# Mixer projections moved into the steps of the latent attention, and the gated products of the expert loop taken one weight tile earlier

## The chip, the core and the metric

One core of one Trainium2 chip. Engines run their own instruction streams and meet through semaphores: TensorE (PE, its weight loads PEld), VectorE (DVE), ScalarE (ACT), GpSimd (POOL), and SyncE (SP), which issues most transfers. The metric is device time in microseconds of one launch, a median of runs.

## What is computed

Two models, one behind the other, on 512 tokens of width 1024. The first has two layers; the second has one, with 32 experts. Only what lies around the change is shown.

```python
def token_mixers(h, cos, sin, w_in, ...):
    proj = h @ w_in
    (sc_b, sc_c, sc_h, gq, gk, gv, gg, ga_f, ga_b, cq, ckv, kr, cfm_in) = jnp.split(proj, ...)
    y_a = sc_b * depthwise_conv(sc_c * sc_h, w_sc_conv)              # 3 taps
    ...  # gated linear attention over gq, gk, gv with decays from ga_f, ga_b -> o
    y_b = o * jax.nn.silu(gg)
    qm = (rms_norm(cq, g_mla_q) @ w_mla_uq)                          # 4 heads of 64 + 32
    kvm = (rms_norm(ckv, g_mla_kv) @ w_mla_ukv)                      # 4 heads of 64 + 64
    y_c = blocked_attention(q_c, k_c, v_c, ...)                      # 4 heads x 4 blocks of 128 queries
    a, gate = jnp.split(cfm_in, 2, axis=-1)
    u = depthwise_conv(a * jax.nn.sigmoid(gate), w_cfm_dw)           # 31 taps
    y_d = jax.nn.silu(layer_norm(u, ...))
    return concatenate(rms_norm of y_a, y_b, y_c, y_d) @ w_out

def run_block(args):                                                 # 128 slots of one expert
    hb = x_pad[toks] @ w1[e] + b1[e]
    g_part = jnp.minimum(hb[..., ::2], 7.0)
    u_part = jnp.clip(hb[..., 1::2], -7.0, 7.0)
    act = g_part * jax.nn.sigmoid(1.702 * g_part) * (u_part + 1)
    return act @ w2[e] + b2[e]
```

## The kernel before

All activations lie channel by channel: a tile is 128 channels by 512 tokens, and hT, the input of a layer, has eight of them. Weights come through one ring of eight tiles of 512 KB (RING, TILE); SP waits for a tile's slot (L393) and loads the next tile (L395). Each program of an engine is one stream in written order, so the order of the lines is the order of the work. Values are named in a table of marks: `when("probs", l, i)` is the count that the semaphore of an engine has reached when that value is there. TensorE's results go to eight banks that are handed out in turn (`bank`); a bank is taken again when the engine that read its last holder has said `free`.

A mixer layer (DEPTH is 2) is ordered like this before the change:

- TensorE (from L627 to L730): the projections of PROJ in the order a0, a1, gate0, gate1, misc (with a second use of its tile, kswap), ckv, cq0, cq1, q, k, then the four banks of gv (two tiles), then b0, b1, c0, c1, h0, h1, gg0, gg1. `project` is eight products of a weight tile with hT. Then the sums of squares of ckv and cq (`norm`), one modulation tile for the second model (`modulation(("kv", l))`, 16 matmuls of two columns), the keys and values of the latent attention (knope, mv), the queries (qh, qswap) and the decays' inputs (la).
- The attention has 16 steps, i = head * 4 + block. In step i TensorE issues the scores of step i + 1, waits for the probabilities of step i and transposes them; after every fourth step it waits for the copied transposes and multiplies them with the values (yc). ScalarE keeps the scores (L1216), takes the exponential (L1220) and copies the transposes of step i - 1 (L1201). VectorE takes the row maximum (L1775), the reciprocal of the row sum (L1778) and scales (L1781).
- VectorE runs the 31 taps of the wide convolution (L1659, two channel tiles, so 62 operations) and the 3 taps of the short one under the projections.
- ScalarE copies each projection out of its bank (`keep`, L1157).
- Behind the attention, TensorE has ten modulation tiles (`modulation(("gla", l, 0))`), while VectorE and ScalarE make the decays and their products for the gated linear attention (from L1785, L1229); TensorE then waits for the first of them (kdec, L1833).

The expert loop has 32 laps, one block of 128 slots each, 24 weight tiles a lap (MOE_TILES). A weight is used as two parts: ScalarE rounds the tile (`round_tile`, L1530) into w_hi, VectorE subtracts that from the tile (`rest_of_tile`, L2311) into w_lo. There are six pairs of them (SPLITS); tile t is rounded when product t - 6 has been made (s_freed). SP may load tile t + 8 when VectorE has done with tile t (s_lo). Products 0 to 7 of a lap fill one pair of banks, 8 to 15 the next; each of them goes through `sigmoid` (L1552) and `swiglu` (L2333 to L2342), is turned by TensorE (act_turned, L1057) in the middle of the eight products that follow, and is split (`round_act`, `rest_of_act`, L2348). Products 16 to 23 use the result. The middle of a lap stands on ScalarE and VectorE like this:

```python
                for t in range(SPLITS, KD + SPLITS):      # 6 to 13
                    rest_of_tile(i, t)
                swiglu(0)                                 # waits for product 7
                for t in range(KD + SPLITS, KD + SPLITS + 2):
                    rest_of_tile(i, t)
                rest_of_act(0)
```

Of the kernel before, what the change touches and what calls it, by code (L numbers as in the profile page):

```python
# [104 lines left out]
SLOT = {n: i for i, n in enumerate(PROJ)}  # L105

# [25 lines left out]
def build(nc, io, marks, found):  # L132
    with ExitStack() as ctx:
# [107 lines left out]
        z_la, cneg, e_la, dtmp = spare("c0"), spare("h0"), spare("cq0"), spare("gate0")  # L241
# [311 lines left out]
        def _(pe):  # L553
# [51 lines left out]
            def used(n=1):  # L605
                state["pending"] += n
# [27 lines left out]
            def project(name, ready=None):  # L634
                w = tile().rearrange("p (k m) -> p k m", m=P)
                chunks(name, lambda k: w[:, k, :], lambda k: hT[:, k, :], KD, ready=ready)
                used()

# [3 lines left out]
            for l in range(DEPTH):  # L642
                project(("proj", l, PROJ[0]), ready=("norm_out", ("in",) if l == 0 else ("ln2", l - 1)))
                for name in PROJ[1:4]:
                    project(("proj", l, name))
                w = tile().rearrange("p (k m) -> p k m", m=P)
                chunks(("proj", l, "misc"), lambda k: w[:, k, :], lambda k: hT[:, k, :], KD)
                chunks(("kswap", l), lambda k: w[:, k, 32:128], lambda k: hT[:, k, :], KD, 96)
                used()
                for name in PROJ[5:10]:  # L650
                    project(("proj", l, name))

                w0 = tile().rearrange("p (k m) -> p k m", m=MIX)
                w1 = tile().rearrange("p (k m) -> p k m", m=MIX)
                for b in range(TB):
                    out = bank("gv", l, b)
                    for k in range(KD):
                        mm(out[:, 0:MIX], hT[:, k, b * P:(b + 1) * P], (w0 if k < 4 else w1)[:, k % 4, :],
                           k == 0, k == KD - 1, *(("gv", l, b) if k == KD - 1 else ()))
                used(2)  # L660
                for name in PROJ[10:]:
                    project(("proj", l, name))
# [36 lines left out]

                pe.wait_ge(dve_done, when("keys", l))  # L700
# [410 lines left out]
        def _(act):  # L1111
# [41 lines left out]
            for l in range(DEPTH):  # L1153
# [6 lines left out]
                keep("a0"), keep("a1"), keep("gate0", ACT.Sigmoid), keep("gate1", ACT.Sigmoid)  # L1160
                keep("misc")
                for i, name in enumerate(("ckv", "cq0", "cq1")):
# [6 lines left out]
                act.wait_ge(pe_done, when("full", "proj", l, "q"))  # L1169
                act.wait_ge(act_done, did.n)  # L1170
                nc.scalar.activation(proj[:, SLOT["q"], :], bank_of("proj", l, "q")[:], ACT.Copy,
                    scale=DK ** -0.5).then_inc(act_done, did.up(("free", "proj", l, "q"), ("proj", l, "q")))
                keep("k")
                for b in range(TB):
                    act.wait_ge(pe_done, when("full", "gv", l, b))
                    act.wait_ge(act_done, did.n)
                    nc.scalar.activation(vtok[:, b, :], bank_of("gv", l, b)[:, 0:MIX], ACT.Copy).then_inc(act_done,
                        did.up(("free", "gv", l, b), ("gv_kept", l, b)))
                for name in PROJ[10:16]:
                    keep(name)  # L1180
# [1381 lines left out]
```

## Time and profile before

| | |
|---|---|
| median of three runs | 3957.78 us (3948.6 to 3963.21) |
| profiled execution | 3951.65 us, span 3949.9 us |
| PE busy | 3554.2 us (90%) |
| PEld busy | 2481.5 us (63%) |
| DVE busy | 2409.6 us (61%) |
| ACT busy | 1733.2 us (44%) |
| POOL busy | 509.8 us (13%) |
| HBM read, written | 588.45 MB, 29.36 MB |

Layer 0 of the first model runs from about 39 to 928 us, layer 1 to about 1818, the second model's mixer to about 2640, and the expert loop from there to the end. Busy time is that of the records; matmuls overlap, so their busy time isn't their pace. A granted clock of 1.00 is 2.4 GHz, 0.50 is 1.2 GHz. The DMA share is the mean over 16 engines. "Idle before" names the time that an engine waited ahead of an instruction, and what ended the wait.

### The profile page before, as it was taken

What the parts mean: (1) busy time and instruction counts of PE and PEld (TensorE: products, weight loads), DVE (VectorE), ACT (ScalarE), POOL (GpSimd) and SP (SyncE); (2) the same over time, 40 slices, a digit from 0 to 9 for tenths busy, and PEclk for the clock granted to TensorE, in tenths of its full rate; (3) what the DMA queues carried; (4) which work ended last, traced back from release to release, by engine and by line L of the source; (5) the groups of instructions that cost most, each with busy time, mean ns of one, the idle gap of its engine ahead of it and who ended that gap; (6) DMA issues with size and microseconds to landing.
All of it is one profiled execution on the core that took longest, in us unless ns stands there. A gap on an engine that the chain in (4) does not pass through costs nothing.

```text
span 3949.9 us, 43762 instructions
## 1 busy us (share of the span) xinstructions
PE 3554.2 (90%) x13692; PEld 2481.5 (63%) x13692; DVE 2409.6 (61%) x2911; ACT 1733.2 (44%) x2333; POOL 509.8 (13%) x625
## 2 busy tenths in 40 slices
PE   7978799999978799997888899959999999999996
PEld 3437468874437468875554554457777777777774
DVE  5334355654334355653335774168888898988885
ACT  2134132332144142333221113047787877777874
POOL 0000000000000000000000000023434343434340
PEclk9975799999975899997999999979999999999998
DMA  4202123322202122322111002259999999999994
GB/s 172 74 16 80 53 75 96 96 91 69 75 16 80 55 76 94 96 91 75 38 42 48 22 1 91 75 192 339 345 336 346 336 362 332 353 332 349 335 354 161
DMA packets 167840, 619.37 MB, mean 157 GB/s; under 512 B 18512, under 2 KB 18640, under 8 KB 167024
## 3 DMA queue, kind: packets, MB, share of 16 engines
q1 hardware_dynamic: 156768, 573.84, 40.8%
q0 software_dynamic: 10960, 44.04, 4.0%
q8 instruction: 70, 1.15, 0.1%
q14 instruction: 42, 0.34, 0.0%
HBM read 588.45 MB, written 29.36 MB: 156 GB/s over the span
## 4 chain that ended last, share of the span: by engine, by line
PE 61%; DVE 15%; DMA 9%; ACT 7%; issue 7%; POOL 0%; DVEq 0%; ACTq 0%; SPq 0%; POOLq 0%
PE bank L569 51%; DMA sb_ring<-in_w 8%; PE bank L1049 7%; DVE w_part L2311 3%; ACT w_part L1530 2%; DVE sb_rstd L1624 2%; DVE sb_work L2338 1%; DVE sb_work L2342 1%; DVE sb_work L2333 1%; PE bank L1057 1%; DVE sb_work L2335 1%; PE bank L1018 1%; ACT sb_work L1220 0%; DVE sb_work L2110 0%; DVE sb_turn_tables L2106 0%
## 5 line engine op out<-in xcount | busy, mean ns | idle before, releaser
L2311 DVE TENSOR_TENSOR w_part<-sb_ring,w_part 128x1024 fp32r<-128x1024 f32 x762 | 894.7, 1223 | 128.2 <-ACT w_part L1530 127.8
L1530 ACT ACTIVATE w_part<-sb_ring 128x1024 fp32r<-128x1024 f32 x762 | 772.5, 1053 | 145.5 <-PE bank L1049 86.3
L1049 PE MATMUL bank<-w_part,xg_hi 128*128 128x512 f32 x2048 | 570.1, 400 | 0.0
L569 PE MATMUL bank<-h_hi,split_part 128*128 128x512 f32 x1408 | 443.5, 400 | 8.3 <-ACT h_hi L1319 8.3
L1049 PEld LDWEIGHTS bank<-w_part,xg_hi 128*128 128x128 f32 x2048 | 387.1, 190 | 90.7
L569 PE MATMUL bank<-sb_work,sb_ring 128*128 128x512 f32 (+4 forms) x864 | 330.3, 538 | 16.5 <-DVE sb_modv L1614 10.5
L1049 PE MATMUL bank<-w_part,xg_lo 128*128 128x512 f32 x1024 | 323.6, 397 | 0.0
L569 PEld LDWEIGHTS bank<-h_hi,split_part 128*128 128x128 f32 x1408 | 267.4, 190 | 74.8 <-issue 8.4
L569 PE MATMUL bank<-sb_work 128*128 128x64 f32 (+6 forms) x992 | 253.2, 461 | 42.1 <-DVE sb_work L1833 22.8
L1049 PE MATMUL bank<-w_part,act_hi 128*128 128x512 f32 x1024 | 284.7, 400 | 0.1
L569 PEld LDWEIGHTS bank<-sb_work,sb_ring 128*128 128x128 f32 (+3 forms) x864 | 163.1, 190 | 179.8 <-issue 159.1
L569 PE MATMUL bank<-sb_hT,sb_ring 128*128 128x512 f32 (+1 forms) x608 | 265.4, 599 | 11.4 <-ACT sb_hT L1140 11.4
L569 PE MATMUL bank<-h_lo,split_part 128*128 128x512 f32 x704 | 272.4, 394 | 0.0
L569 PE MATMUL bank<-act_hi_ff,split_part 128*128 128x512 f32 x704 | 229.0, 407 | 5.7 <-DVE act_lo_ff L1940 5.7
L442 POOL DMA_DIRECT2D sb_work<-in_ctx x1 | 0.6, 592 | 1798.2 <-PE bank L569 1798.2
L569 PEld LDWEIGHTS bank<-sb_work 128*128 128x128 f32 (+3 forms) x992 | 159.1, 248 | 105.9 <-issue 46.0
L1049 PEld LDWEIGHTS bank<-w_part,xg_lo 128*128 128x128 f32 x1024 | 194.6, 190 | 47.1
L1312 ACT ACTIVATE split_part<-sb_ring 128x1024 fp32r<-128x1024 f32 x136 | 142.7, 1052 | 176.7 <-PE bank L569 176.7
L569 PEld LDWEIGHTS bank<-sb_hT,sb_ring 128*128 128x128 f32 (+1 forms) x608 | 115.9, 191 | 158.9 <-issue 156.5
L1049 PEld LDWEIGHTS bank<-w_part,act_hi 128*128 128x128 f32 x1024 | 187.5, 188 | 40.0 <-issue 0.5
L490 POOL TENSOR_TENSOR sb_work<-sb_work 128x1 f32<-128x1 f32 x126 | 97.3, 773 | 666.8 <-ACT sb_work L1588 394.0
L1348 ACT ACTIVATE sb_work<-bank 128x512 f32<-128x512 f32 x88 | 52.8, 600 | 294.8 <-PE bank L569 294.8
(331 smaller groups left out, 5055.9 us busy)
## 6 DMA issues: line engine op xcount, KB each, us to landing
sb_ring<-in_w SPq DMA_DIRECT2D x768, 512.0 KB, 7.1
sb_ring<-in_wstream SPq DMA_DIRECT2D x304, 512.0 KB, 3.5
y_rows<-sb_padc POOLq DMA_DIRECT2D x1, 4096.0 KB, 27.6
sb_xT<-in_x SPq DMA_DIRECT2D x1, 2048.0 KB, 11.5
x_rows<-sb_padc SPq DMA_DIRECT2D x1, 2048.0 KB, 22.6
residual<-sb_hT POOLq DMA_DIRECT2D x1, 2048.0 KB, 7.7
sb_hT<-residual POOLq DMA_DIRECT2D x1, 2048.0 KB, 8.0
x_rows<-sb_work SPq DMA_DIRECT2D x1, 2048.0 KB, 12.6
```

The lines of the kernel that those rows point to most:

```text
L490: nc.gpsimd.tensor_tensor(passed[:, n:n + 1], slot_row[:, 0:1], slot_row[:, 0:1], ALU.add).then_inc(moe_pool_done, turn_did.up())
L569: ins = nc.tensor.matmul(out, l, r, start=start, stop=stop)
L1018: ins = nc.tensor.transpose(out[:, k * P:(k + 1) * P], block_rows[:, (half * 4 + k) * P:(half * 4 + k + 1) * P], ident)
L1049: ins = nc.tensor.matmul(out[n][:], l[:, k, :], r[:, n * 512:(n + 1) * 512], start=False, stop=(k, p) == (KD - 1, 2))
L1057: ins = nc.tensor.transpose(banks[6 + half][:, k * P:(k + 1) * P], u_part[:, half, k * P:(k + 1) * P], ident)
L1312: nc.scalar.activation(split_hi[t % NSPLIT], ring[:, n % RING, :], ACT.Copy).then_inc(act_done, did.up(("w_hi", l, t)))
L1348: nc.scalar.activation(ubuf[:, i % 4, 1:T + 1], bank_of("up", l, c, v)[:], ACT.Copy).then_inc(act_done, did.up(("free", "up", l, c, v), (" ...
L1530: nc.scalar.activation(w_hi[t % SPLITS], ring[:, t % RING, :], ACT.Copy).then_inc(s_hi, 1)
L1624: nc.vector.reciprocal(out, out).then_inc(dve_done, did.up())
L2311: nc.vector.tensor_tensor(w_lo[t % SPLITS], ring[:, t % RING, :], w_hi[t % SPLITS].bitcast(F32), ALU.subtract).then_inc(s_lo, 1)
L2333: nc.vector.tensor_scalar(g_part, pairs[:, :, 0], SWIGLU_LIMIT, None, ALU.min).then_inc(moe_dve_done, turn_did.up(("g_part", half)))
L2335: nc.vector.tensor_scalar(u, pairs[:, :, 1], SWIGLU_LIMIT, -SWIGLU_LIMIT, ALU.min, ALU.max).then_inc(moe_dve_done, turn_did.up())
```

## The change

In the mixers, `project` now takes its weight tile by name, so that tiles can be used out of order. Ahead of the attention stand only ckv, cq0, cq1, misc, a0, the two norms' sums, then a1, gate0, gate1. The projection q goes right ahead of step 0, and the other ten stand in steps 0 to 8, 14 and 15 (BESIDE_AT), between the scores of step i + 1 and the wait for the probabilities of step i; gv takes two steps with two banks each. ScalarE keeps them one step later, ahead of copying the transposes (`keep_beside`); gg0 and gg1 it keeps behind the last step. The modulation tile goes into step 10. VectorE's 31 wide taps go into the steps, two taps (four operations) each, behind the scaling; the products of c and h and the short taps go into steps 11 to 14, and the product with b behind step 15. The buffer z_la moves from c0's place to the last two tiles of sq.

In the expert loop, `sigmoid` and `swiglu` of either half go ahead of one more weight tile: ahead of tile 13 and tile 21, which stood before them until now.

```diff
+GV_TILE = 10
+BESIDE_AT = {0: "k", 1: "gv0", 2: "gv2", 3: "c0", 4: "h0", 5: "c1", 6: "h1", 7: "b0", 8: "b1", 14: "gg0", 15: "gg1"}
+MOD_STEP = 10
...
-        z_la, cneg, e_la, dtmp = spare("c0"), spare("h0"), spare("cq0"), spare("gate0")
+        z_la, cneg, e_la, dtmp = sq[:, 6:8, :], spare("h0"), spare("cq0"), spare("gate0")
...
+            def project(l, name, ready=None):
+                i = SLOT[name]
+                w = loaded(in_layer + i + (2 if i >= GV_TILE else 0)).rearrange("p (k m) -> p k m", m=P)
+                chunks(("proj", l, name), lambda k: w[:, k, :], lambda k: hT[:, k, :], KD, ready=ready)
+                if name == "misc":
+                    chunks(("kswap", l), lambda k: w[:, k, 32:128], lambda k: hT[:, k, :], KD, 96)
                 used()
...
+                in_layer = state["stream"]
+                project(l, "ckv", ready=("norm_out", ("in",) if l == 0 else ("ln2", l - 1)))
+                for name in ("cq0", "cq1", "misc", "a0"):
+                    project(l, name)
                 norm(("kv", l), sq, 0, 1, ones, center=False)
                 norm(("q", l), sq, 1, 2, ones_mix, center=False)
+                for name in ("a1", "gate0", "gate1"):
+                    project(l, name)
+                state["stream"] = in_layer + len(PROJ) + 2
-                modulation(("kv", l))
...
+                project(l, "q")
                 pe.wait_ge(dve_done, when("keys", l))
...
                     if i + 1 < HEADS * TB:
                         scores(i + 1)
+                    if i in BESIDE_AT:
+                        if BESIDE_AT[i][:2] == "gv":
+                            token_values(l, int(BESIDE_AT[i][2]))
+                        else:
+                            project(l, BESIDE_AT[i])
+                    if i == MOD_STEP:
+                        modulation(("kv", l))
                     pe.wait_ge(dve_done, when("probs", l, i))
...
                     if i >= 1:
+                        if i - 1 in BESIDE_AT and BESIDE_AT[i - 1][:2] != "gg":
+                            keep_beside(i - 1)
                         turned_out(i - 1)
                 turned_out(HEADS * TB - 1)
+                keep("gg0", ACT.Silu), keep("gg1", ACT.Silu)
...
                         ALU.mult).then_inc(dve_done, did.up(("probs", l, i)))
+                    dve.wait_ge(dve_done, did.n)
+                    wide_taps(2 * i, min(2 * i + 2, CFM_TAPS))
+                    if i == HEADS * TB - 1:
+                        did.note("norm_in", ("cfm", l))
+                    if i == MOD_STEP + 1:
+                        modulated(("kv", l))
...
+                    if MOD_STEP + 1 < i < MOD_STEP + 5:
+                        dve.wait_ge(dve_done, did.n)
+                        short_taps(i - MOD_STEP - 2)
...
-                for t in range(SPLITS, KD + SPLITS):
+                for t in range(SPLITS, KD + SPLITS - 1):
                     rest_of_tile(i, t)
                 swiglu(0)
-                for t in range(KD + SPLITS, KD + SPLITS + 2):
+                for t in range(KD + SPLITS - 1, KD + SPLITS + 2):
                     rest_of_tile(i, t)
                 rest_of_act(0)
-                for t in range(KD + SPLITS + 2, 2 * KD + SPLITS):
+                for t in range(KD + SPLITS + 2, 2 * KD + SPLITS - 1):
                     rest_of_tile(i, t)
                 swiglu(1)
-                rest_of_tile(i, 2 * KD + SPLITS)
+                for t in range(2 * KD + SPLITS - 1, 2 * KD + SPLITS + 1):
+                    rest_of_tile(i, t)
                 rest_of_act(1)
```

ScalarE's loop changes in the same way, with round_tile and sigmoid.

## Rows read from the trace of the kernel before

**Rows 1.** The page, part 4: the chain that ended last, shares of the span

```profile
PE 61%; DVE 15%; DMA 9%; ACT 7%; issue 7%; POOL 0%; DVEq 0%; ACTq 0%; SPq 0%; POOLq 0%
```

**Rows 2.** Windows: stretch, length, busy of PE, PEld, DVE, ACT, POOL, clock, DMA, GB/s

```profile
39.00:186.00 147.00, 146.65 (x369) 70.50 (x370) 65.89 (x105) 23.38 (x37) 0.00 (x0) 0.98 0.20 68
...
217.15:294.30 77.15, 53.54 (x126) 20.48 (x124) 21.52 (x49) 35.20 (x68) 0.00 (x0) 0.71 0.04 14
1108.90:1183.00 74.10, 54.31 (x132) 21.40 (x130) 21.50 (x49) 35.69 (x69) 0.00 (x0) 0.70 0.04 15
```

**Rows 3.** Groups by form, 100 to 170 us: busy us, mean ns of one

```profile
L569 PE MATMUL bank<-sb_hT,sb_ring 128*128 128x512 f32 x132 | 57.0, 592 | 0.0
```

**Rows 4.** Timeline, 184 to 222 us: start, us, then the idle time before

```profile
186.76 1.28 ACT L1124 ACT_TABLE_LOAD   x1
...
188.06 1.49 ACT L1124 ACTIVATE sb_rstd<-bank,sb_consts 128x512 f32<-128x512 f32 x2
...
188.78 3.35 DVE L1624 RECIPROCAL sb_rstd<-sb_rstd 128x512 f32<-128x512 f32 x1 [9.81 <-ACT sb_rstd L1124]
...
193.18 5.32 PE L569 MATMUL bank<-sb_work,sb_ring 128*64 128x512 f32 x8 [2.87 <-DVE sb_work L1642]
```

**Rows 5.** Timeline, one attention step of layer 0

```profile
280.81 0.60 ACT L1216 ACTIVATE sb_work<-bank 128x512 f32<-128x512 f32 x1
280.86 0.66 PE L710 MATMUL bank<-sb_consts,sb_work 128*128 128x128 f32 x4 [1.80 <-DVE sb_work L1781]
...
281.44 0.69 DVE L1775 TENSOR_REDUCE sb_work<-sb_work 128x1 f32<-128x512 f32 x1 [0.64 <-ACT sb_work L1216]
282.17 0.72 ACT L1220 ACTIVATE sb_work<-sb_work 128x512 f32<-128x512 f32 x1 [0.75 <-DVE sb_work L1775]
...
283.28 0.49 DVE L1781 TENSOR_SCALAR sb_work<-sb_work 128x512 f32<-128x512 f32 x1
```

**Rows 6.** Timeline, VectorE: the wide convolution's taps behind the first

```profile
71.63 39.84 DVE L1659 SCALAR_TENSOR_TENSOR sb_work<-sb_padc,sb_cols,sb_work 128x512 f32<-128x512 f32 x60
```

**Rows 7.** Timeline behind the attention: modulation tiles, and the decay chain's ends

```profile
294.30 29.37 PE L569 MATMUL bank<-sb_csil,sb_ring 128*128 128x2 f32 x160
...
302.37 1.36 ACT L1229 ACTIVATE sb_work<-sb_work 128x512 f32<-128x512 f32 x2 [7.37 <-DVE sb_work L1790]
...
319.75 2.56 DVE L1833 SCALAR_TENSOR_TENSOR sb_work<-sb_work 128x1024 f32<-128x1024 f32 x2
```

**Rows 8.** Windows of the expert loop, columns as in rows 2

```profile
3000.77:3040.73 39.96, 37.70 (x173) 30.23 (x172) 35.58 (x37) 31.21 (x36) 16.64 (x20) 1.00 0.95 342
3022.00:3030.00 8.00, 8.00 (x37) 6.44 (x36) 7.78 (x8) 7.76 (x10) 0.34 (x1) 1.00 0.67 203
3000.00:3022.00 22.00, 19.75 (x93) 15.64 (x92) 20.52 (x23) 15.85 (x20) 14.23 (x17) 1.00 1.02 396
2640.00:3877.00 1237.00, 1173.25 (x5292) 940.78 (x5291) 1102.70 (x1120) 968.27 (x1086) 493.69 (x589) 0.99 0.95 342
```

**Rows 9.** Timeline of one lap: VectorE's idle moments and one gated product

```profile
3001.97 1.23 DVE L2311 TENSOR_TENSOR w_part<-sb_ring,w_part 128x1024 fp32r<-128x1024 f32 x1 [0.34 <-ACT w_part L1530]
...
3003.11 0.68 DVE L2333 TENSOR_SCALAR sb_work<-bank 128x512 f32<-128x512 f32 x1
...
3005.25 0.69 DVE L2342 TENSOR_TENSOR sb_work<-sb_work 128x512 f32<-128x512 f32 x1
...
3014.78 1.23 DVE L2311 TENSOR_TENSOR w_part<-sb_ring,w_part 128x1024 fp32r<-128x1024 f32 x1 [0.17 <-ACT w_part L1530]
...
3020.14 0.69 DVE L2348 TENSOR_TENSOR act_lo<-bank,act_hi 128x512 fp32r<-128x512 f32 x1 [0.24 <-ACT act_hi L1558]
...
3023.38 6.90 DVE L2311 TENSOR_TENSOR w_part<-sb_ring,w_part 128x1024 fp32r<-128x1024 f32 x6 [0.22 <-ACT w_part L1530]
```

**Rows 10.** Waits in the expert loop, 2640 to 3895 us: total, times, longest

```profile
PE bank L1057 <- DVE sb_work L2342: 66.6, 63, 2.3
...
DVE w_part L2311 <- ACT w_part L1530: 117.9, 161, 2.1
```

More of the change, by code:

```diff
@@ L632, in running, with token_values @@
                 mm(state[kind][:], ones_d, src[:, k, :], k == 0, k == KD - 1, *((kind, tag) if k == KD - 1 else ()))
-            def project(name, ready=None):
-                w = tile().rearrange("p (k m) -> p k m", m=P)
-                chunks(name, lambda k: w[:, k, :], lambda k: hT[:, k, :], KD, ready=ready)
-                used()
+            def project(l, name, ready=None):
[4 more added lines that the diff above has]
+                    chunks(("kswap", l), lambda k: w[:, k, 32:128], lambda k: hT[:, k, :], KD, 96)
+                used()
+            def token_values(l, first):
+                if first == 0:
+                    state["gv"] = [loaded(in_layer + GV_TILE + i).rearrange("p (k m) -> p k m", m=MIX) for i in range(2)]
+                w0, w1 = state["gv"]
+                for b in range(first, first + 2):
+                    out = bank("gv", l, b)
+                    for k in range(KD):
+                        mm(out[:, 0:MIX], hT[:, k, b * P:(b + 1) * P], (w0 if k < 4 else w1)[:, k % 4, :],
+                           k == 0, k == KD - 1, *(("gv", l, b) if k == KD - 1 else ()))
+                if first > 0:
+                    used(2)
             pe.wait_ge(s_in, 16 * 5)
@@ L1158, in keep @@
                         **kw).then_inc(act_done, did.up(("free", "proj", l, name), ("proj", l, name)))
-                keep("a0"), keep("a1"), keep("gate0", ACT.Sigmoid), keep("gate1", ACT.Sigmoid)
-                keep("misc")
                 for i, name in enumerate(("ckv", "cq0", "cq1")):
@@ L1168, in _ @@
                     keep(name)
[L1169 to L1180, printed above, removed]
-                keep("gg0", ACT.Silu), keep("gg1", ACT.Silu)
+                keep("misc")
+                keep("a0")
                 deviation(("kv", l), scale=1.0 / P)
                 deviation(("q", l))
+                keep("a1"), keep("gate0", ACT.Sigmoid), keep("gate1", ACT.Sigmoid)
                 for h in range(HEADS):
@@ L1209, in turned_out, with keep_beside @@
                             ACT.Copy).then_inc(act_done, did.up(("free", "yc", l, h), ("yc", l, h)))
+                def keep_beside(i):
+                    name = BESIDE_AT[i]
+                    if name[:2] == "gv":
+                        for b in range(int(name[2]), int(name[2]) + 2):
+                            act.wait_ge(pe_done, when("full", "gv", l, b))
+                            act.wait_ge(act_done, did.n)
+                            nc.scalar.activation(vtok[:, b, :], bank_of("gv", l, b)[:, 0:MIX],
+                                ACT.Copy).then_inc(act_done, did.up(("free", "gv", l, b), ("gv_kept", l, b)))
+                    else:
+                        keep(name)
+                keep("q", scale=DK ** -0.5)
                 for i in range(HEADS * TB):
@@ L1650, in conv @@
                 n = len(dst)
-                for j in range(taps):
+                for j in taps:
                     for c in range(n):
@@ L1772, in _, with wide_taps, short_taps @@
                         ALU.add).then_inc(dve_done, did.up(("free", "la", l, d)))
+                for c in range(2):
+                    dve.wait_ge(act_done, when("proj", l, f"gate{c}"))
+                    dve.wait_ge(dve_done, did.n)
+                    nc.vector.tensor_tensor(padc[:, c, 15:T + 15], proj[:, SLOT["a0"] + c, :], proj[:,
+                        SLOT["gate0"] + c, :], ALU.mult).then_inc(dve_done, did.up())
+                def wide_taps(j0, j1):
+                    conv([proj[:, SLOT["a0"] + c, :] for c in range(2)], lambda c: padc[:, c], range(j0, j1),
+                         lambda c, j: col(l, "cfm_w", c * CFM_TAPS + j))
+                def short_taps(j):
+                    conv([y[:, c, :] for c in range(2)], lambda c: pads[:, c], (j,),
+                         lambda c, j: col(l, "sc_w", c * 3 + j))
                 for i in range(HEADS * TB):
```

61 lines of the change are left out of this document (16 added, 45 removed).

## The prediction

> **What bounds the kernel now.** I read the chain that ended last first [rows 1]: TensorE holds 61% of it, VectorE 15%, and 9% is weight loads of the expert loop. So two places are worth a look: where TensorE's line is broken in the mixers, and where the loop waits.
>
> Mixers: the table by stretches of layer 0 [rows 2] shows projections with TensorE busy all of 147 us at a granted clock of 0.98, and then attention, 77.15 us in layer 0 and 74.10 in layer 1, with 53.5 busy at a clock of 0.71. The reader is to see both losses: 24 us idle, and much of the busy time at the lower of the two levels. The steps themselves are a chain [rows 5]: keep the scores (0.60), row maximum (0.69), exponential (0.72 and its read-out), scaling (0.49), transposes (0.66), then the next.
>
> Loop: 1237 us hold 31 laps of 39.9 us, with a DMA share of 0.95, TensorE busy 1173.25 us (94.8%) and VectorE 1102.70 (89.1%) [rows 8]. The waits [rows 10] name all that TensorE waited for there: 66.6 us for the gated product (L2342), 2.15 us a lap. VectorE waited 117.9 us (3.8 a lap) for rounded tiles. Three resources stand close together, so removing TensorE's wait need not be worth 2.15.
>
> **The change part by part, mixers.** I count one layer from 39.0 us to the start of the ten modulation tiles, 294.3 us: 255.3 us.
>
> One projection is 16 matmuls; 132 of them took 57.0 us [rows 3], so 6.9 us each. Before, 21 such units (two of them the value tiles, and one the second use of misc) give 144.9 of the 146.65 us [rows 2], with 1.8 for the cold start. After, nine stand ahead (ckv, cq0, cq1, misc twice, a0, a1, gate0, gate1): 62.1 + 1.8, and six matmuls of the two norms by the same row, 2.6: 66.5 us.
>
> The norms' square root, reciprocal (3.35 each) and scaling (0.7 each) left a hole [rows 4]: TensorE idles 2.87 before L569 at 193.18 and then runs eight matmuls in 5.32 us that take 3.4 at the full clock. After, a1, gate0 and gate1 (20.7 us) cover table load, root, two reciprocals and three scalings (1.3 + 1.4 + 6.7 + 2.2 = 11.6), so I cost them at nothing; without cover they would be 7 us. From 193.18 to the first kept score, 217.15, were 24.0 us; less 1.9 of cold clock 22.1. Then comes q, 6.9. So far 95.5 us.
>
> The steps: scores 0.86 (two matmuls), a projection 6.9, transposes about 0.5 apart, since they pipeline. That is 8.3 us on TensorE. Beside it VectorE has four taps at 0.66 (39.84 over 60) [rows 6], the maximum, a short reciprocal and the scaling, 4.0 us, and ScalarE some 2.7 (four operations of the kinds in [rows 5]). Both fit, so steps 0 to 8 take nine times 8.3, 74.3 us. Steps 3 and 7 add the head's values, 3.4 at full clock, and about 1.0 of waiting for the copied transposes, which stand behind a kept projection on ScalarE: 8.8.
>
> Steps 9 to 13 have no projection. Here the added taps do cost: VectorE must finish 2.7 us of them before the next maximum. Its loop is 2.7 + 0.7 + 0.8 + 0.9 = 5.2, where a step before took about 4.5. Steps 9 and 10 together 4.6 (the first is ready, and the modulation tile, 2.9 by the ten tiles' row [rows 7], runs beside). Step 11 takes 5.5 to its transposes; its values and step 12, behind the two products of pads (1.4), about 10; step 13 3.5. That makes 23.5, and 28 if the clock falls as it does in the steps now. I take 26. Steps 14 and 15: 8.3 + 7.4 + 1.0 + 3.4, and 2.5 for a cold first projection: 22.6. Steps together 131.7.
>
> New layer 95.5 + 131.7 = 227.2 against 255.3: 28.1 saved; layer 1, whose attention was 3.05 shorter, 25.0. Both 53.
>
> What is late next: after the steps the ten modulation tiles take 29.4 us, and the decay chain ends at 319.75 + 2.56 = 322.3, before the tiles' end at 323.7 [rows 7]. The chain starts from the last head's copy on ScalarE, as before; y's two products and the last taps run on VectorE under the values. But gg0 and gg1 with Silu now stand on ScalarE ahead of the decay's exponential: load 1.28, two copies 1.2, load 1.28, 3.8 us, inside the 7.37 us that ScalarE idled there. Nothing, then, with 1.4 us of slack behind it. The Trainium skill (ScalarE: Activation LUTs, What ACT_TABLE_LOAD costs) adds a drain of 1.38 us to every load of 1.28, which would speak against the extra switch. In this trace the root starts 0.02 us after its load ended (188.06 against 186.76 + 1.28) [rows 4], so the row decides; by the page 6.5 us would stand there, still inside.
>
> Of weight loads, the change moves order alone: the same tiles are asked of SP's queue, and in the steps, where the DMA share is now 0.04 [rows 2]. No cost.
>
> **The loop.** Product 7 frees both the slot that tile 13 is rounded into and the banks that the gated product reads. Before, rounding (1.06) and the rest on VectorE (1.23) of tile 13, and of tile 21, came first; now the product does, 2.85 us from the first minimum to the last multiplication (3003.11 to 3005.94) [rows 9]. If TensorE alone decided, its 2.15 us a lap [rows 10] would go. But VectorE does the same work: between its tile 12 and tile 24 it is full but for idle moments of 0.34, 0.17, 0.24 and 0.22 [rows 9], which the order closes, since each was a wait for ScalarE, and the gated product now fills it. That is 0.97 a lap. What starts a lap is tile 12 landing, and its load is issued when VectorE ends tile 4 of that lap, so VectorE's 0.97 is carried on through the ring. The other bound is TensorE's 2.15. The low bound is a loss, below. I take 1.0, nearest to VectorE's rows, because VectorE issues what DMA waits for: 31 laps, 31 us.
>
> Also late in this order: tile 13 and 21 are finished 2 to 2.7 us later, and the loads into their slots with them. Behind the waiting multiplication on VectorE are tiles 13 to 15; TensorE wants tile 13 three products later, and they are 1.4 us each.
>
> **Sum.** 53 + 31 = 84 us from the profiled 3951.65 (span 3949.9): 3868. The median of the runs shown is 6.1 higher, 3957.78, so I predict 3874.
>
> **Rivals.**
> - The loop doesn't move. For it: DMA is 1.02 in the full stretch (396 GB/s) and 0.95 over all [rows 8], so at most 2.7 us a lap is slack, and none if its low stretch is latency that comes back. Against: in that low stretch (0.67, 203 GB/s, 8 us) loads wait for VectorE. Time 3957.8 - 53 = 3905.
> - The loop gains all of TensorE's wait, 66.6. For: TensorE's own work is 37.7 in the lap from 3000.77 [rows 8] and it has no other wait. Against: of VectorE's 3.8 us of idle time a lap, 1.7 would then be all that is left beside its work of 35.6 to 36, and only 0.97 of it has a cause that goes away. 3957.8 - 53 - 67 = 3838. The Trainium skill (DMA: Bandwidth & Descriptors, Anatomy of one DMA) gives bytes over 436 GB/s for data movement; 342 GB/s over 39.9 us would then need 31 us and leave TensorE the bound, which is this rival. The full stretches here show 396, so the page's rate isn't reached, and the trace speaks half for it.
> - The steps don't hold their projections at full clock, or transposes and copies wait in the other engines' new order: a third of the mixer's gain, 18, with the loop's 31: 3909.
> - Slower: the ring starves. The ring has eight tiles; the loads behind tiles 13 and 21 go out 2.85 us later, right ahead of the stretch where DMA is already at 0.67. If the queue runs dry for it, each lap pays 2.85 and not 0: 88 us against 53, 3957.8 + 35 = 3993. It decides from the point where the load behind tile 21, then issued at about 3018.9, comes after the full stretch has ended; that stretch reaches to 3022 [rows 8], which leaves 3 us, some two tiles of 1.3 us at 396 GB/s.
> - The change doesn't do what it says: TensorE runs in order, and a projection put between scores and transposes only lengthens a step by its 6.9 if the chain of the next step can't run under it. Then all is moved, nothing hidden, and the taps come on top: 3950. Against: scores of step i+1 are issued ahead of the projection, and everything they need is two steps old.
>
> **How the numbers follow.** Forecast 0.42 (its own range 3850 to 3895); loop unmoved 0.22; full loop 0.14; steps a third 0.10; starved ring 0.06; nothing hidden 0.06. The range takes in the loop unmoved and the steps' third, with the mixer's bounds of 35 to 60 us (all cold in steps 9 to 13 on the one side, values unwaited on the other), and half of the full loop: 3843 to 3915. 0.5% is about what a measurement of this kernel can tell, some 20 us: faster 0.88, same 0.06, slower 0.06.
>
> **What would show it.** Right: the distance from the layer's first projection to the modulation tiles near 227 us, granted clock near 1 over steps 0 to 8 and falling in 9 to 13, steps at 8.3 us; no hole before L569's first keys; the wait for the last decay product unchanged. In the loop: TensorE's wait for the gated product under 1 us a lap, a lap of 38.9, VectorE's small idle moments gone, DMA share 0.97 or more. Wrong: VectorE's taps ahead of a maximum with TensorE idle in steps 0 to 8; the modulation tiles followed by a wait; laps of 39.9 with ScalarE waiting longer for tiles (DMA), or above 40 with the low DMA stretch longer (starved).

## The result and the profile after

The changed kernel takes 3822.1 us, median of 4 runs (3815.6 to 3830.2), against 3956.9 for the kernel before (4 runs, 3948.6 to 3963.2): a ratio of 0.967, with an interval of 0.9644 to 0.9697. The forecast was 3874 with a range of 3843 to 3915. So the direction was right and the size was not: the time lies 52 us below the forecast and 21 below the range.

The profiled execution took 3815.60 us (span 3813.8), 136.1 less than the profiled 3951.65 of before. Two stamps of the expert loop divide this sum. The first is the first gated product, the second the last one of a first half. The rows are the answer for that line in the kernel before and then after: operation and count, shortest/median/longest in ns, first and last start. The last start is that of a second half; the last first half starts at 3877.0 before and at 3743.1 after.

```profile
L2333 DVE TENSOR_SCALAR sb_work<-bank x64: 678/684/686, 2642.8 to 3891.3; 128x512 f32<-128x512 f32 x64
```

```profile
L2361 DVE TENSOR_SCALAR sb_work<-bank x64: 676/682/687, 2589.5 to 3755.7; 128x512 f32<-128x512 f32 x64
```

The loop begins 53.3 us earlier, which is the mixers' part (forecast 53). From there the first halves' products of the 32 turns are 1234.1 us apart before and 1153.6 after: 39.81 us a lap against 37.21, 2.60 less, 80.6 over 31 laps (forecast 31). The last 2.2 lie behind them. The error is in the loop.

**Mixers.** Windows of the changed kernel, columns as in [rows 2]. In order: the projections ahead of the attention; the norms' stretch with a1, gate0 and gate1 in it; steps 0 to 8; steps 9 to 12; the last steps.

```profile
39.00:106.00 67.00, 66.97 (x151) 28.96 (x152) 25.83 (x35) 17.20 (x25) 0.00 (x0) 0.97 0.17 55
106.00:142.46 36.46, 36.46 (x90) 15.19 (x89) 18.25 (x29) 8.90 (x17) 0.00 (x0) 1.00 0.18 58
142.46:218.00 75.54, 73.67 (x229) 39.07 (x228) 35.75 (x61) 22.89 (x45) 0.00 (x0) 1.00 0.18 56
218.00:244.00 26.00, 15.04 (x55) 7.32 (x54) 16.47 (x30) 9.89 (x20) 0.00 (x0) 0.74 0.12 41
244.00:265.45 21.45, 20.76 (x52) 8.63 (x50) 12.94 (x22) 4.02 (x8) 0.00 (x0) 0.92 0.14 43
```

Against the attention of [rows 2], where TensorE was busy 53.54 of 77.15 us at a granted clock of 0.71, the reader sees nine steps in which it is busy 73.67 of 75.54 us at 1.00. The hole of [rows 4] is gone (36.46 of 36.46). The loss sits where the steps have no projection: 11 us idle, clock 0.74.

**Behind the attention.** Timeline rows that answer to [rows 7]: start, length, then the idle time before.

```profile
265.45 31.65 PE L572 MATMUL bank<-sb_csil,sb_ring 128*128 128x2 f32 x160
266.22 1.28 ACT L1169 ACT_TABLE_LOAD   x1
267.51 1.28 ACT L1169 ACTIVATE sb_work<-bank 128x512 f32<-128x512 f32 x2
268.88 1.28 ACT L1245 ACT_TABLE_LOAD   x1
...
273.51 1.35 ACT L1245 ACTIVATE sb_work<-sb_work 128x512 f32<-128x512 f32 x2 [3.35 <-DVE sb_work L1818]
...
290.88 2.56 DVE L1861 SCALAR_TENSOR_TENSOR sb_work<-sb_work 128x1024 f32<-128x1024 f32 x2
...
296.95 8.66 PE L572 MATMUL bank<-sb_work 128*128 128x64 f32 x40
```

The two gate copies and two table loads stand in ScalarE's idle time, of which 3.35 us remain of 7.37. The decay chain ends at 293.4, the modulation tiles at 297.1: TensorE goes on without a wait. But the tiles themselves last 31.65 us, where they lasted 29.37.

**Loop.** Windows, columns as in [rows 2]: the whole loop, and one lap, to be read against the last and the first row of [rows 8].

```profile
2588.00:3743.00 1155.00, 1153.42 (x5278) 938.41 (x5277) 1096.26 (x1118) 961.26 (x1085) 448.83 (x586) 1.00 1.00 365
2963.00:3000.07 37.07, 37.07 (x171) 30.24 (x170) 35.28 (x37) 30.92 (x36) 14.26 (x19) 1.00 1.00 368
```

TensorE is busy 99.9% of the time, DMA has a share of 1.00 (0.95 before), VectorE 94.9% (89.1%). The waits of the loop, in total us, times, longest, answer to [rows 10]:

```profile
PE bank L1069 <- DVE sb_work L2370: 1.2, 3, 0.6
```

66.6 us have become 1.2. The timeline of one lap, beside [rows 9], shows the product ahead of a tile (2963.05 to 2965.88), and the transposes of the activation coming when its result is there, with no idle time before them:

```profile
2963.05 0.68 DVE L2361 TENSOR_SCALAR sb_work<-bank 128x512 f32<-128x512 f32 x1
...
2965.19 0.69 DVE L2370 TENSOR_TENSOR sb_work<-sb_work 128x512 f32<-128x512 f32 x1
2965.80 3.49 DVE L2339 TENSOR_TENSOR w_part<-sb_ring,w_part 128x1024 fp32r<-128x1024 f32 x3
...
2967.01 0.60 PE L1069 MATMUL bank<-sb_consts,sb_work 128*128 128x128 f32 x4
```

### The profile page after: what moved, and what is told of

It is laid out like the page before. It is cut to its first block, busy times and chain, and to the rows that moved or that the text cites. A ratio compares the mean times of both kernels' runs of the same rounds, so it can differ in the third digit from the quotient of the medians.

```text
span 3813.8 us, 43797 instructions
## 1 busy us (share of the span) xinstructions
PE 3506.0 (92%) x13692; PEld 2476.4 (65%) x13692; DVE 2405.6 (63%) x2911; ACT 1727.9 (45%) x2334; POOL 465.9 (12%) x625
## 4 chain that ended last, share of the span: by engine, by line
PE 54%; issue 20%; POOL 10%; DVE 8%; ACT 4%; POOLq 2%; DMA 1%; SPq 0%; DVEq 0%; ACTq 0%
PE bank L572 53%; POOL pick L538 2%; DVE sb_rstd L1640 2%; POOL sb_work L493 2%; POOL y_rows L544 1%; POOL sb_work L499 1%; POOL picks_e L500 1%; POOL sb_work L530 1%; POOLq L506 1%; POOL sb_work L532 1%; POOLq L505 1%; DVE sb_work L2138 0%; DVE sb_turn_tables L2134 0%; POOL sb_work L527 0%; DVE sb_work L2162 0%
## 5 line engine op out<-in xcount | busy, mean ns | idle before, releaser
L572 PE MATMUL bank<-sb_work 128*128 128x64 f32 (+6 forms) x992 | 231.6, 438 | 45.8 <-DVE sb_work L1861 22.8
L1926 DVE TENSOR_TENSOR split_part<-sb_ring,split_part 128x1024 fp32r<-128x1024 f32 x136 | 165.8, 1220 | 19.9 <-ACT split_part L1328 19.8
```

The lines of the kernel that those rows point to most:

```text
L572: ins = nc.tensor.matmul(out, l, r, start=start, stop=stop)
L1926: nc.vector.tensor_tensor(split_lo[t % NSPLIT], ring[:, n % RING, :], split_hi[t % NSPLIT].bitcast(F32), ALU.subtract).then_inc(dve_done, ...
```

## The experiments

Two theories stand against each other in the expectations. **T**: TensorE sets the lap, and the lap lost exactly the time for which TensorE had stood before the activation's transposes. **V**: VectorE's order sets it, by way of the ring: a tile landing at the start of a lap, its load issued when VectorE frees the slot. A lap below is the mean distance of first halves' products over 31 laps of one profiled execution. Four kernels with the new loop order (after, its repetition, e2 and e5) have means of 37.21, 37.32, 37.23 and 37.41 and the same median, 37.08, so 0.2 in a mean says little and the median is given where it matters. A gap is the distance from the start of the last matmul ahead of the transposes to the first of them, less the 0.23 us at which matmuls follow each other.

**The two parts alone.** The loop's edits undone in the changed kernel, and the loop's edits alone in the kernel before.

```diff
 e1: the changed kernel with the loops of ScalarE and VectorE as before (the edits below, backwards)
 e2: the kernel before, with these edits
-                for t in range(SPLITS, KD + SPLITS):
+                for t in range(SPLITS, KD + SPLITS - 1):
 (and the other three ranges of the change, on both engines)
```

> The changed kernel with the expert loop's order as it was; the mixers' part stays. The question is how the 136 us that the profiled executions differ by (3951.65 to 3815.60) divide. The first gated product of the loop starts 53.3 us earlier in the changed kernel (2642.84 against 2589.52), so both theories expect 53 us less than the kernel before, a ratio of 0.9865, laps of 39.8 us again and a DMA share of 0.95 in the loop. If the ratio is under 0.98, some of what I put down to the loop belongs to the mixers.

> The kernel before with the loop's new order alone. Theory T (TensorE is the clock of a lap: its products, 37.1 us, plus the gaps between starts ahead of its transposes, 1.87 and 0.71 us beyond the usual 0.23) expects laps of 37.1 to 37.2 and 80 us less, a ratio of 0.980. Theory V (the prediction's: VectorE's idle moments of 0.97 a lap, passed on through the ring) expects laps of 38.9 and 31 us less, 0.992; under it the missing 50 us would have to come from the mixers' part.

Before was 3945.2 (7 runs) here. Mixers alone: 3896.9, ratio 0.9876 (0.9860 to 0.9893), 48 us less; its lap is 39.70. Loop alone: 3874.1, ratio 0.9824 (0.9808 to 0.9841), 71 us less, and a lap of 37.23 against 39.81. The two gains, 119 us, are less than the 135 of both together above (130 when the changed kernel was run again, below), and each interval reaches some 7 us to either side; the profiled executions give 45 for the start of the loop in e1 (2598.1) and 80 for the laps in e2. The mixers' forecast of 53 is met within these bounds, on their low side. The loop's part is less than T's time by about 10 us and far more than V's 31: V as the prediction had it has fallen.

**The halves of the loop.** The product of the first half moved alone (e3), and of the second alone (e4).

```diff
 e3
-                for t in range(SPLITS, KD + SPLITS):
+                for t in range(SPLITS, KD + SPLITS - 1):
                     rest_of_tile(i, t)
                 swiglu(0)
-                for t in range(KD + SPLITS, KD + SPLITS + 2):
+                for t in range(KD + SPLITS - 1, KD + SPLITS + 2):
 e4
-                for t in range(KD + SPLITS + 2, 2 * KD + SPLITS):
+                for t in range(KD + SPLITS + 2, 2 * KD + SPLITS - 1):
                     rest_of_tile(i, t)
                 swiglu(1)
-                rest_of_tile(i, 2 * KD + SPLITS)
+                for t in range(2 * KD + SPLITS - 1, 2 * KD + SPLITS + 1):
+                    rest_of_tile(i, t)
```

> The kernel before with only the first half's gated product (and its sigmoid) one weight tile earlier. Theory T: the gap of 1.87 us ahead of the first half's transposes goes and the 0.71 of the second stays: laps of 37.9, 58 us less, ratio 0.985. Theory R (the ring: the gain is only there when both halves fill the stretch in which the DMA engines are at 0.67, since loads wait for VectorE there): less than the half's own gap, laps near 39, 25 us less, 0.994.

> The kernel before with only the second half's gated product one weight tile earlier. Theory T: the 0.71 us gap goes: laps of 39.1, 22 us less, ratio 0.9944. Theory R: the second half stands right ahead of the stretch where DMA is at 0.67 (3022 to 3030 in the lap shown), so this half gives the larger part: laps of 38.5 or less, 40 us or more, under 0.990.

e3: ratio 0.9872 (0.9854 to 0.9891), lap 38.03. e4: 0.9934 (0.9917 to 0.9951), lap 38.91. The waits of the loop, first of e3, then of e4:

```profile
PE bank L1057 <- DVE sb_work L2342: 23.1, 32, 1.4
```

```profile
PE bank L1057 <- DVE sb_work L2342: 44.8, 30, 2.1
```

| kernel | lap, us | gap, first half | gap, second half |
|---|---|---|---|
| before | 39.81 | 1.69 | 0.70 |
| e3, first half moved | 38.03 | 0.02 | 0.88 |
| e4, second half moved | 38.91 | 1.56 | 0.00 |
| after | 37.21 | 0.03 | 0.03 |

Each half takes its own gap away and the lap follows: -1.78 and -0.90, together -2.68 against -2.60 for both. The parts add up. The gaps together fall by 1.49 in e3 (where the second half's grows by 0.18), by 0.83 in e4 and by 2.33 in the changed kernel. Most of what e3 and the changed kernel gain beyond that is the clock. In the 31 laps of the kernel before, TensorE's granted clock is at the lower level, 0.50, in four short stretches, 13.7 us in all; one of them:

```profile
2966.00:2969.00 3.00, 3.00 (x8) 2.32 (x8) 2.88 (x4) 1.99 (x2) 2.85 (x5) 0.50 1.07 407
```

At half speed 13.7 us cost 6.9 us, 0.22 a lap. e4 has four such stretches too, e3 and the changed kernel have none in these laps. With 0.22 added where they went, the sums are 1.71, 0.83 and 2.55 against laps shorter by 1.78, 0.90 and 2.60. That speaks for T.

**Less to load, in both kernels.** Every fourth tile of the expert loop is loaded by half (512 of 1024 columns), so an eighth of the weights is not read, and the output is not the reference's. If the lap waits for data, it shortens.

```diff
+                n = TILE // 2 if t % 4 == 0 and signal is s_lo else TILE
-                sp.dma_start(ring[:, t % RING, :], src).then_inc(s_tile[t % RING], 16)
+                sp.dma_start(ring[:, t % RING, 0:n], src[:, 0:n]).then_inc(s_tile[t % RING], 16)
```

> The kernel before with only half of every fourth weight tile loaded in the expert loop (the output is then not the reference's): 6 half tiles a lap, 1.57 of some 13.6 MB, 12% of a lap's traffic. The step of the prediction that is on trial said that a lap starts when its tile 12 lands. If it does, the lap of 39.8 us shortens by at least half of the 4 us of traffic, to 38 or less. Theory T (TensorE's work and its two gaps make the lap; the DMA stretch at 0.67 is only what they leave over): laps stay at 39.7 to 39.8, and the DMA share falls to 0.84.

> The same cut of traffic in the changed kernel, where the DMA share stands at 1.00. Theory T: laps stay at 37.1, the share falls to about 0.9. Theory D (the changed loop has come down to the DMA engines' limit, and TensorE only just keeps up): laps fall below 36.8, as far as VectorE's 35.3 lets them.

One run each, beside 3951.2 for the kernel before. In the changed kernel: 3812.6 us, lap 37.07, TensorE busy throughout with a DMA share of 0.96. In the kernel before: 3897.6 us, lap 38.15 (median 38.10), the first half's gap down from 1.69 to 0.25, the second's unmoved (0.70 and 0.73). All 31 laps then lie between 38.08 and 38.67, where those of the kernel before reach from 38.56 to 41.48. The same 900 us (2700 to 3600) of four kernels, columns as in [rows 2]: before, before with less to load, after, after with less to load.

```profile
2700.00:3600.00 900.00, 851.58 (x3846) 682.77 (x3844) 801.99 (x815) 707.42 (x794) 355.74 (x426) 1.00 0.95 342
```

```profile
2700.00:3600.00 900.00, 884.81 (x4011) 709.75 (x4010) 835.64 (x849) 738.34 (x828) 372.83 (x445) 1.00 0.93 315
```

```profile
2700.00:3600.00 900.00, 898.42 (x4113) 730.83 (x4112) 853.62 (x872) 750.06 (x848) 348.54 (x462) 1.00 1.00 366
```

```profile
2700.00:3600.00 900.00, 900.00 (x4130) 734.24 (x4129) 856.81 (x876) 751.49 (x851) 351.17 (x464) 1.00 0.96 326
```

So T falls too, in its plain form: it said that data had no part in the gap of the kernel before. ScalarE's waits for tiles in that stretch, before and then with less to load, name what it was:

```profile
ACT w_part L1530 <- DMA sb_ring<-in_w: 45.1, 34, 2.3
```

```profile
ACT w_part L1531 <- DMA sb_ring<-in_w: 0.8, 1, 0.8
```

The first half's gap was for the greater part a late tile: a rounding whose tile had not landed stood ahead of the sigmoid and of the product in two queues that run in order. Of the 43 such waits of the whole loop before (58.1 us), 30 (38.1 us) are at tile 13 and the other 13 (20.0 us) at tile 12. The second half's gap was order alone, since less data left it as it was. The change takes both out of TensorE's way. For tile 13 it does so not by making the tile land earlier (in the mean of 30 laps it lands 1.6 us behind product 7's end before, 1.25 after) but by no longer having it stand ahead: TensorE takes it up only five products later. Tile 12 still stands ahead of the product; it now lands 2.1 us ahead of product 7's end instead of 1.2, and 3 waits at it are left (4.1 us).

**Less for TensorE.** Of each group of eight products, the third of the three partial products is left out for six tiles, in the changed kernel: 8.3 us less of TensorE a lap.

```diff
                     for p, (l, r) in enumerate(((left_hi, hi), (left_hi, lo), (left_lo, hi))):
+                        if p == 2 and 0 < k < KD - 1:
+                            continue
```

> The changed kernel without the third product (low part of the activations by the high part of the weight) for six of the eight tiles of each of the three groups, so its output is not the reference's: 36 matmuls fewer a lap, 8.3 us of TensorE. It shows what stands next behind TensorE. If the DMA engines at share 1.00 are at their limit, laps stay at 37.0 with the share at 1.00 or above. If the share of 1.00 still has room, VectorE's 35.3 us of work come next: laps of 35.5 to 36.5, with VectorE at 97% or more.

```profile
2700.00:3600.00 900.00, 753.67 (x3211) 593.13 (x3211) 851.47 (x864) 742.01 (x842) 355.01 (x456) 0.94 0.99 364
```

One run: 3822.4 us and a lap of 37.48 (median 37.50, 0.42 longer than with the full work). TensorE now waits 135.1 us in 900 before the transposes, at a granted clock of 0.94, and the lap is as long as ever. So behind TensorE there stand, within 0.4 us of it, the loads and VectorE (851.47 of 900, 94.6%). Which of these two holds this lap isn't shown. It leans to the loads: ScalarE's waits for tiles rise from 15.1 us (44 times) to 43.7 (121 times) in these 900 us, and of VectorE's 48.5 idle us 38.4 are waits for rounded tiles. A run with less to load and less for TensorE together would tell; there is none. The Trainium skill (DMA: Bandwidth & Descriptors, Where 436 GB/s comes from) gives about 358 GB/s as the limit of one core between HBM and SBUF. The trace does not settle it for the steady rate: of the 366 GB/s over 900 us in the changed kernel 352 are reads (317 of 330 MB) and the rest are writes. Over the 22 us of [rows 8] it was exceeded: of the 396 GB/s the weights alone are 372.

**More for VectorE, at three places.** A memset of 0.91 us, with its waits, behind the second gated product (e6), three of them there (e7), and one at the lap's end (e10).

```diff
 e6, e7 (one, three)
                 swiglu(1)
+                for n in range(1):
+                    nc.vector.memset(rstd[:, 0:2, :], 0.0).then_inc(moe_dve_done, turn_did.up())
+                    dve.wait_ge(moe_dve_done, own_turn(i, turn_did))
 e10
                     for t in range(MOE_TILES, MOE_TILES + SPLITS):
                         rest_of_tile(i, t)
+                    nc.vector.memset(rstd[:, 0:2, :], 0.0).then_inc(moe_dve_done, turn_did.up())
```

> The changed kernel with one more VectorE operation a lap (a memset of 1024 columns, some 0.9 us, behind the second half's gated product). Theory T (TensorE is the clock, VectorE has 1.8 us of idle time a lap left): laps stay at 37.1 to 37.2. Theory V (VectorE feeds the ring, and what it does more is passed on): laps of 38.0, 28 us more in the whole.

> The same with three such operations, 2.7 us and their waits for one another. VectorE's work is then 38.1 to 38.4 us a lap. Theory T: TensorE's 37.1 is passed and VectorE takes over, laps of 38.2 to 38.6, TensorE waiting 1.1 to 1.5 us a lap. Theory V: laps of 39.9, 2.8 above the changed kernel.

> The changed kernel with one memset of 0.91 us a lap on VectorE, as in the run that had it behind the second gated product and lost 1.3 us a lap, but now at the lap's end, behind the low part of tile 29, where VectorE idles 1.47 us. Theory T with slack by place: laps stay at 37.1 to 37.2. If VectorE's total work feeds the ring whatever the place, laps grow to 38.0 or more again.

| kernel (one run each but for after) | us | lap, mean / median |
|---|---|---|
| after | 3822.1 | 37.21 / 37.08 |
| e6, 0.91 behind the product | 3869.2 | 38.71 / 38.42 |
| e7, three times 0.91 behind the product | 3988.0 | 42.55 / 42.15 |
| e10, 0.91 at the lap's end | 3823.0 | 37.47 / 37.19 |

The waits of TensorE in the loop, in e6 and then in e7:

```profile
PE bank L1061 <- DVE act_lo L2376: 36.1, 32, 2.2
```

```profile
PE bank L1061 <- DVE act_lo L2376: 97.2, 30, 3.7
```

The same work costs 1.3 to 1.5 us a lap at the one place and 0.1 to 0.3 at the other. In VectorE's queue it takes more than its record: from the start of the product's last multiplication to the next tile it is 0.61 us in the changed kernel and 1.89 in e6, so one memset and its waits are 1.28 us, and three are 3.66 (4.27). The first place thus has little or no slack: the median lap grew by 1.34 for the 1.28. What is delayed there is the low part of the activation (L2376), which the next products need; in the changed kernel it stands two tiles behind the product. Three cost 5.1 to 5.3 a lap: the 3.66, and TensorE's clock, granted at 0.94 over 2700 to 3600 instead of 1.00. In the 31 laps it is at the lower level for 143 us, which at half speed cost up to 2.3 us a lap. Neither theory had expected this: T said 37.1 to 37.2 for e6, V 38.0. VectorE's idle share says nothing about it: its slack is a matter of place.

**The steps' projections spread out, and the changed kernel once more.**

```diff
-BESIDE_AT = {0: "k", 1: "gv0", 2: "gv2", 3: "c0", 4: "h0", 5: "c1", 6: "h1", 7: "b0", 8: "b1", 14: "gg0", 15: "gg1"}
+BESIDE_AT = {0: "k", 1: "gv0", 3: "gv2", 4: "c0", 6: "h0", 7: "c1", 9: "h1", 10: "b0", 12: "b1", 14: "gg0", 15: "gg1"}
```

> The changed kernel with the five steps that have no projection spread out: 2, 5, 8, 11 and 13 instead of 9 to 13. If a step without a projection is long only because it follows another one (VectorE's taps then stand ahead of the next maximum, while behind a projection the chain has run ahead), each costs TensorE's own 1.4 us, and the 118.3 us from the first to the last transposes of layer 0 become 105 to 108: 20 to 26 us less than the changed kernel in both layers, near 3800 on its scale. If every such step costs its chain of 5.2 us wherever it stands, the distance stays at 116 or more and the gain is under 5 us.

> The changed kernel itself, on the same chip as the run with the spread steps, so that the two can be compared: ratio 0.967 to the kernel before, as measured.

3802.3 us (3799.0 to 3804.3), ratio 0.9614 (0.9595 to 0.9634), against 3821.7 and 0.9664 (0.9642 to 0.9686) for the changed kernel on the same chip: 19.3 us less, a little under the 20 to 26 expected, and the fastest version here. From the first transposes of the steps to the last it takes 104.9 us instead of 118.3. Windows of the steps, first after, then e5, columns as in [rows 2]:

```profile
142.00:265.50 123.50, 109.98 (x335) 55.24 (x333) 65.32 (x113) 37.03 (x74) 0.00 (x0) 0.93 0.16 51
```

```profile
142.00:252.00 110.00, 105.05 (x335) 54.07 (x333) 65.20 (x113) 36.90 (x74) 0.00 (x0) 1.00 0.18 57
```

The work is the same (335 matmuls, 113 and 74 operations); the clock granted is 1.00 instead of 0.93, and TensorE idles 5 us instead of 13.5. No plain step stands next to another.

## Why the prediction was right, and where it was wrong

**Projections and norms: right.** The first transposes (142.30) start 103.3 us behind the layer's first projection (39.03). Forecast were 95.5, and 7.8 for the scores and the projection of step 0: the same. The three scalings and two reciprocals are covered, as costed.

**Steps 0 to 8: right.** Transposes follow each other at 8.17 to 8.21 us (8.3), and at 12.95 where a head's values are added (8.3 + 4.4).

**Steps 9 to 13: right in size, and in cause for the half of it.** The transposes of steps 8 and 13 are 26.1 us apart (26 chosen between 23.5 and 28), at a clock of 0.74. The parts are 4.6 for steps 9 and 10 (4.6 forecast), 5.0 for step 11 (5.5), 13.2 for its values and step 12 (10), and 3.3 for step 13 (3.5). So the 26 has some luck in it: the 2.5 chosen on top for the clock stand for 3.2 that are missing in one part. The chain of waits through the first of them, start, length, what, is VectorE's taps ahead of a maximum, as said:

```profile
221.85 2.74 DVE sb_work L1675 x4
224.59 0.61 DVE sb_work L1783
225.22 0.82 ACT sb_work L1233 x2
226.34 0.50 DVE sb_work L1789
226.86 2.74 DVE sb_work L1675 x4
```

The longest single wait, 5.51 us before the values at 233.50, has a link that the prediction did not name. ScalarE copies step 11's transposes (L1201) only behind the exponential of step 12, and that one waits for a maximum behind VectorE's taps and the two products of pads.

**The layer's sum: right.** From first projection to modulation tiles 226.4 us in layer 0 (227.2) and 225.5 in layer 1, where 255.0 and 250.7 were: 28.5 and 25.2 saved (28.1, 25.0). Not foreseen was that the tiles behind would last 2.3 and 2.0 us longer, so 26.3 and 23.2 are left at their end. The loop still starts 53.3 us earlier, 3.8 more than these two give. Its start scatters by as much: 2640.9 to 2645.0 us in five kernels with the mixers of before, 2588.7 to 2598.1 in those with the mixers of after and the same steps. So the 53 is met, but not to the microsecond that the agreement suggests.

**Behind the attention: right.** ScalarE's gates and table loads cost nothing. The activation behind the Silu load starts at 267.51, 0.01 after the load's end at 267.50, so the row that was used (0.02 in [rows 4]) held here as well. The Trainium skill's further drain of 1.38 us (ScalarE: Activation LUTs, What ACT_TABLE_LOAD costs) doesn't show in the trace of the kernel after either.

**The loop: wrong.** The step that failed is "I take 1.0, nearest to VectorE's rows", and both terms behind it were mis-sized. The first is VectorE's idle time between tile 12 and tile 24, "0.97 a lap". It was read from one lap. There the stretch took 22.98 us, and 22.0 was to be left; over 30 laps it took 23.87 in the mean before and 21.95 after, so 1.92 a lap went. In the lap of [rows 9] the late tile was tile 12 (ScalarE waits 1.82 us for it and 0.50 for tile 13), which falls ahead of the stretch; in most laps it is tile 13, inside it. The second is the way back, from tile 24 to tile 12 of the next lap. "What starts a lap is tile 12 landing" carried it on unchanged, 16.8 in that lap; in the mean it was 15.97 and became 15.26, 0.71 less. Together 2.63, where 2.60 were measured. In the way back lies the stretch of [rows 8] with the DMA share at 0.67; from the issue of tile 12's load to its rounding it was 8.83 us in the mean, and is 8.14. I had named this stretch (loads there wait for VectorE) and argued against the unmoved loop with it, but then took the transit of the load as fixed in my own sum. Without TensorE's stops the same loads are asked for in a shorter lap: 342 GB/s became 365. What set the lap was TensorE's work and its two gaps, as e2, e3 and e4 show. The loads entered it through the late tile in the first gap: with less to load the median lap is 38.10, and 37.07 of work with the gaps of 0.25 and 0.73 make 38.05.

**The rival of the full loop (0.14): right in kind, under-priced.** It gave 3838, and the time is 3822. It took TensorE's wait as the 2.15 us a lap that the waits list [rows 10]. The table counts idle time from the end of a matmul's record, and a record of 0.39 us is followed, when nothing is waited for, by the next start after 0.23. So each of the two waits is 0.16 short: in the lap of [rows 9] they are 1.71 and 0.55, 2.26 together, while by starts it is 1.87 + 0.71 = 2.58. Over all laps the starts give 2.39, of which 0.06 are left after the change. The rest of the measured 2.60 is the clock but for 0.05: the four stretches at 0.50 of the kernel before, 0.22 a lap, are gone in the kernel after, and e3 and e4, one without them and one with, bear it out. The Trainium skill (Perfetto Trace Analysis, Tensor Engine Instruction) says that the end of a matmul in the profile is computed from its size and not observed. The rows fit this: records overlap by 0.16 us in a full stream.

**The chances.** The full loop deserved at least the chance of my own case. For it spoke that TensorE had no other wait and 37.7 us of work a lap; against it I set VectorE's need of 35.6 to 36 us and DMA's 0.95, and both fit into 37.2. Nothing in the rows forbade it; "only 0.97 of it has a cause that goes away" rested on the one lap. With its price mended (31 times 2.33 is 72, and 7 for the clock, which it could not know), it gives 3826.

**The other rivals.** The loop unmoved (0.22, 3905): laps are 37.2, not 39.9. Only a third of the mixers' gain (0.10) and nothing hidden (0.06): the nine steps run at clock 1.00 and 8.2 us. The starved ring (0.06, 3993): the loads behind tiles 13 and 21 do go out later, by 1.2 and 1.1 us against product 7's end and not by 2.85, but the next ones go out 1.5 us earlier, and ScalarE's wait for tiles in 900 us fell from 45.1 to 15.1 us, as the rows show, the first of them above:

```profile
ACT w_part L1546 <- DMA sb_ring<-in_w: 15.1, 44, 2.3
```

**What stays open.** Whether the loads or VectorE hold the lap of 37.5 us when TensorE has less to do, and why the granted clock fell for those four stretches of the loop before. That 12% less to load left the changed lap at 37.07 (median 37.07 against 37.08) shows that TensorE is the bound there; the 37.5 shows that it is so by very little.

## What to carry to other kernels

In a queue that runs in order, an operation placed behind one that waits for data inherits that wait: move the one that the busiest engine needs ahead, even where the time table says that the engine issuing it has little slack. When you price such a move, count waits over all laps and not in one, follow the loop round with every term free to shrink, and take the gap of the bound engine from start to start. Spread short dependent steps without cover among covered ones; two in a row cost idle time and clock at once.

## What the runs showed of the hardware

- Keeping TensorE busy ahead of sparse work didn't carry over into it. The ten modulation tiles of layer 0, 160 matmuls of two columns, took 29.37 us before and 31.65 after, though the 21.45 us just ahead of them had a clock of 0.69 before and 0.92 after. The granted clock over the tiles themselves fell from 0.59 to 0.55, first before, then after:

```profile
294.30:323.67 29.37, 29.37 (x162) 29.37 (x161) 22.21 (x27) 13.81 (x27) 0.00 (x0) 0.59 0.54 161
```

```profile
265.45:297.10 31.65, 31.65 (x162) 31.65 (x162) 22.20 (x27) 17.57 (x31) 0.00 (x0) 0.55 0.48 153
```

- A DMA share of 1.00 is not by itself a bound, and it doesn't follow the bytes. With an eighth less of the weights to load, the changed kernel moved 326 GB/s instead of 366, the share fell only to 0.96, and the median lap went from 37.08 to 37.07.
- A record's length isn't what an operation costs its queue when it waits for the one before: a memset of 0.91 us took 1.28 us of VectorE's queue in e6, and three took 3.66 in e7.
- Two bounds stood within half a microsecond in a lap of 37.2: TensorE's own work 37.07, and 37.5 for the loads or VectorE once 8.3 us were off TensorE.
